# The 31-tap convolution of the forget-gate mixer: two of four channel tiles as blocked matmuls from shifted copies

## The reference, cut to what matters

```python
def conformer_conv(p_d, dw_w, dw_b, cn_g, cn_b):
    h = p_d[..., :D_D] * jax.nn.sigmoid(p_d[..., D_D:])
    h = causal_dwconv(h, dw_w) + dw_b
    h = layer_norm(h, cn_g, cn_b)
    return jax.nn.silu(h)

def odd_mixer(x, w_in, forget_b, dw_w, dw_b, cn_g, cn_b, w_out):
    p = x @ w_in
    ...
    log_f = jax.nn.log_sigmoid((p[..., 3 * D_C:3 * D_C + H_C] + forget_b).astype(jnp.float32))
    y_c = forgetting_attention(q, k, v, log_f).reshape(bsz, s, D_C)
    y_d = conformer_conv(p[..., 3 * D_C + H_C:], dw_w, dw_b, cn_g, cn_b)
    return jnp.concatenate([y_c, y_d], axis=-1) @ w_out
```

## Time and profile before

| | us |
|---|---|
| Median of 3 runs (2263.66 to 2265.57) | 2264.3 |
| The profiled execution | 2262.41 |
| Its span, first to last instruction | 2260.6 |
| TensorE busy | 2217.2 |
| VectorE busy | 1095.9 |
| ScalarE busy | 780.9 |
| GpSimd busy | 1002.0 |

### The profile page before, as it was taken

One profiled execution on the slowest core, in us unless ns is written; L12 is line 12 of the kernel. 1 busy time (PEld: TensorE's weight loads), 2 busy tenths in 40 slices (PEclk: granted clock), 3 DMA queues, 4 the chain that ended last, 5 costly groups with the idle time before them and its releaser, 6 DMA issues.

```text
span 2260.6 us, 25021 instructions
## 1 busy us (share of the span) xinstructions
PE 2217.2 (98%) x10111; PEld 1787.7 (79%) x10111; DVE 1095.9 (48%) x1693; ACT 780.9 (35%) x1033; POOL 1002.0 (44%) x318
## 2 busy tenths in 40 slices
PE   8999999999999999999999999999999999999998
PEld 6667888888777778888878888888878667888887
DVE  7535034455467451444557321444569725035455
ACT  2453223332344332333322232333336573223331
POOL 3223445554332343554545644536533334444553
PEclk9999999999999999999999999999999999999999
DMA  4122333232212222333333332333313113234332
GB/s 176 57 94 93 131 112 116 108 140 103 93 60 91 75 103 84 130 131 118 116 112 106 113 112 92 120 124 130 131 50 117 66 57 122 105 114 145 105 116 78
DMA packets 36994, 239.91 MB, mean 106 GB/s; under 512 B 4104, under 2 KB 5256, under 8 KB 10384
## 3 DMA queue, kind: packets, MB, share of 16 engines
q1 hardware_dynamic: 35712, 236.20, 29.1%
q10 hardware_dynamic: 1168, 2.11, 0.3%
HBM read 236.18 MB, written 2.11 MB: 105 GB/s over the span
## 4 chain that ended last, share of the span: by engine, by line
PE 85%; DVE 11%; ACT 2%; issue 1%; POOL 1%; DMA 0%; DVEq 0%; SPq 0%; ACTq 0%
PE bank L1147 17%; PE bank L1149 16%; PE bank L1148 16%; PE bank L1447 4%; PE bank L1448 4%; PE bank L1446 4%; PE bank L1197 3%; PE bank L1199 3%; PE bank L1198 3%; DVE bank L2353 3%; PE bank L1342 2%; PE bank L1337 2%; PE bank L1338 2%; DVE X L1950 1%; PE bank L1659 1%
## 5 line engine op out<-in xcount | busy, mean ns | idle before, releaser
L974 POOL TENSOR_TENSOR wlo<-raw,whi 128x2048 fp32r<-128x2048 f32 (+4 forms) x152 | 713.7, 4698 | 578.9 <-ACT whi L573 569.0
L1147 PE MATMUL bank<-XH,whi 128*128 128x512 f32 x1720 | 678.1, 394 | 6.6 <-POOL wlo L1042 6.1
L1149 PE MATMUL bank<-XH,wlo 128*128 128x512 f32 x1720 | 670.8, 390 | 0.0
L1148 PE MATMUL bank<-XL,whi 128*128 128x512 f32 x1720 | 670.3, 390 | 0.0
L1147 PEld LDWEIGHTS bank<-XH,whi 128*128 128x128 f32 x1720 | 323.4, 188 | 87.3 <-issue 15.0
L573 ACT CAST whi<-raw 128x2048 fp32r<-128x2048 f32 (+4 forms) x152 | 289.0, 1903 | 297.7 <-PE bank L1147 162.2
L1149 PEld LDWEIGHTS bank<-XH,wlo 128*128 128x128 f32 x1720 | 323.3, 188 | 67.9
L1148 PEld LDWEIGHTS bank<-XL,whi 128*128 128x128 f32 x1720 | 323.6, 188 | 64.9
L1011 POOL TENSOR_TENSOR AL<-AS,AH 128x1024 fp32r<-128x1024 f32 x40 | 123.6, 3090 | 345.0 <-ACT AH L622 345.0
L2035 DVE TENSOR_TENSOR HF<-sil,bank 128x512 f32<-128x512 f32 x56 | 38.5, 688 | 457.8 <-PE bank L1149 457.8
L1446 PE MATMUL bank<-whi,AH 128*128 128x512 f32 x448 | 174.3, 389 | 0.0
(11 more groups left out here) (298 smaller groups left out, 2952.6 us busy)
## 6 DMA issues: line engine op xcount, KB each, us to landing
raw<-w_ffn_gu SPq DMA_DIRECT2D x88, 1024.0 KB, 4.9
raw<-w_ffn_st SPq DMA_DIRECT2D x56, 1024.0 KB, 4.9
GB<-gb SPq DMA_DIRECT2D x8, 1024.0 KB, 6.9
raw<-w_ffn_dn SPq DMA_DIRECT2D x8, 1024.0 KB, 5.0
raw<-w_diff_in SPq DMA_DIRECT2D x6, 1280.0 KB, 5.6
raw<-w_ev_in SPq DMA_DIRECT2D x6, 1024.0 KB, 5.0
raw<-w_od_in SPq DMA_DIRECT2D x4, 1536.0 KB, 6.4
raw<-w_mla_pair SPq DMA_DIRECT2D x4, 1088.0 KB, 5.6
```

The lines of the kernel that those rows point to most:

```text
L974: pool.tensor_tensor(wlo[:, off:off + size], raw[:, off:off + size], whi[:, off:off + size].bitcast(F32), ALU.subtract).then_inc(lo_ready, 1)
L1147: release(pe.matmul(out, whi[:, off:off + P], xh, start=start, stop=False))
L1148: pe.matmul(out, whi[:, off:off + P], xl, start=False, stop=False)
L1149: return pe.matmul(out, wlo[:, off:off + P], xh, start=False, stop=stop)
```

## The change

Tiles 0 and 1 now both go to TensorE, in another form, and tiles 2 and 3 stay with VectorE (62 taps in place of 93). For each of the two tiles ScalarE issues 16 DMAs (`spread_taps`) that copy `fz` into `ZS`: partition group j of 32 gets the channels of group g shifted by j tokens, for every g. GpSimd makes the weights (`tap_weights`): 32 blocks of 128 x 32, each four small diagonals one above the other, for four taps of 32 channels. TensorE then does 8 blocks of four plain f32 matmuls (`conv_blocks`), one for each group of 32 output partitions, each contracting four taps at once. The 32nd tap is zero. The diagonals, their ring, and the high and low parts of z and of the weights go.

The order changes with it. TensorE: GLU unit, tile 0, GLU unit, tile 1, three-tile unit. ScalarE: both copies of z with their 16 issues each ahead of the cast of the second GLU unit, the cast of the three-tile unit ahead of the gate rows. GpSimd: the weights behind the first and the second GLU unit, the three-tile unit ahead of `diagonal_biases(0)`. VectorE: no taps before glu(2), then 22, glu(3), 9, and 5, 6 and 6 ahead of the three copies; 14 are left for the slots. The LayerNorm's steps all stand one slot earlier (rows in 4 to 6, the scaling at the end of slot 7, columns in 8 and 9, Silu in 10). Constants and parameters gain the columns that `tap_weights` reads.

```diff
-GLU_BANKS = ((0, 1), (0, 1), (2, 0), (1, 2))
+GLU_BANKS = ((0, 1), (0, 1), (0, 1), (2, 3))
-DIAGONALS = 4
+BLOCKED = 2
+TAP_BLOCKS = 8
+SPAN = 4 * (TAP_BLOCKS - 1) + S
...
+        TD = [sb(f"TD{i}", [P, 32, 32], F32, idle) for i in range(BLOCKED)]
+        stack = cons[:, CCOL["stack"]:CCOL["stack"] + 32]
+        ZS = [sb(f"ZS{i}", [P, 4, SPAN], F32, idle) for i in range(BLOCKED)]
-        dg = [sb(f"dg{i}", [P, 2 * P], F32R, ph) for i in range(DIAGONALS)]
...
@@ ScalarE
-            def diagonals(ks):
-                for k in ks:
-                    if k >= DIAGONALS:
-                        act.wait_ge(dg_used, k - DIAGONALS + 1)
-                    d = dg[k % DIAGONALS]
-                    act.activation(d[:, 0:P], ident, ACT.Copy, scale=cwH[:, k:k + 1].bitcast(F32))
-                    act.activation(d[:, P:2 * P], ident, ACT.Copy, scale=cwL[:, k:k + 1]).then_inc(dg_ready, 1)
+            def spread_taps(i):
+                act.wait_ge(z_kept, i + 1)
+                for j in range(4):
+                    for g in range(4):
+                        act.dma_start(ZS[i][32 * j:32 * j + 32, g, :], fz[i][32 * g:32 * g + 32, j:j + SPAN]).then_inc(zs_in[i], 16)
...
-            act.wait_ge(gz_done, 1)
-            act.copy(fz[1][:, PADC:], bank[5][:]).then_inc(z_kept, 1)
-            act.wait_ge(gz_done, 2)
-            act.copy(fzH[:, PADC:], bank[6][:]).then_inc(z_high, 1)
-            act.wait_ge(cw_lo, 1)
-            diagonals(range(0, 20))
+            act.wait_ge(z_padded, 1)
+            for e, b in ((0, 6), (1, 5)):
+                act.wait_ge(gz_done, e + 1)
+                act.copy(fz[e][:, PADC:PADC + S], bank[b][:]).then_inc(z_kept, 1)
+                spread_taps(e)
             split_w()
...
             sigmoid(2)
-            diagonals(range(20, 24))
+            keep_conv(0, blocks_done, 1)
+            split_w()
             act.wait_ge(cum_ready, 1)
             act.dma_start(gate_rows, cum[:]).then_inc(rows_out, 16)
-            diagonals(range(24, TAPS))
             act.wait_ge(rows_out, 16)
             gate_biases(0)
-            keep_conv(1, conv_done, 1)
-            keep_conv(0, dg_used, TAPS)
-            split_w()
             sigmoid(3)
             split_w()
-            keep_conv(2, conv_done, 2)
+            keep_conv(1, blocks_done, 2)
+            keep_conv(2, conv_done, 1)
...
@@ GpSimd
-            split_w(4)
+            def tap_weights(i):
+                pool.tensor_tensor(TD[i][:], stack.unsqueeze(1).to_broadcast([P, 32, 32]),
+                                   pcol_block("taps", i).unsqueeze(2).to_broadcast([P, 32, 32]), ALU.mult).then_inc(td_ready, 1)
+            split_w(3)
+            tap_weights(0)
+            split_w()
+            tap_weights(1)
+            split_w()
...
             diagonal_biases(0)
-            split_w(2)
+            split_w()
             diagonal_biases(1)
...
@@ TensorE
-            def conv_taps(ks):
-                for k in ks:
-                    pe.wait_ge(dg_ready, k + 1)
-                    d, z = dg[k % DIAGONALS], slice(k, k + S)
-                    pe.matmul(bank[7][:], d[:, 0:P], fzH[:, z], start=k == 0, stop=False)
-                    pe.matmul(bank[7][:], d[:, 0:P], fzL[:, z], start=False, stop=False)
-                    pe.matmul(bank[7][:], d[:, P:2 * P], fzH[:, z], start=False, stop=k == TAPS - 1).then_inc(dg_used, 1)
+            def conv_blocks(i):
+                b = CONV_BANK[i]
+                pe.wait_ge(td_ready, i + 1)
+                pe.wait_ge(zs_in[i], 256)
+                claim(b)
+                for k in range(TAP_BLOCKS):
+                    for g in range(4):
+                        ins = pe.matmul(bank[b][32 * g:32 * g + 32, :], TD[i][:, 4 * k + g, :], ZS[i][:, g, 4 * k:4 * k + S],
+                                        start=k == 0, stop=k == TAP_BLOCKS - 1)
+                ins.then_inc(blocks_done, 1)
...
-                for e, b in ((1, 5), (0, 6)):
+                for e, b in ((0, 6), (1, 5)):
...
             tile_end(ins, 2)
-            pe.wait_ge(z_low, 1)
-            claim(7)
-            conv_taps(range(0, 16))
             unit_into(GLU_BANKS[2])
-            conv_taps(range(16, TAPS))
-            freed[3], freed[4], freed[5], freed[7] = ((conv_kept, n) for n in (4, 1, 3, 2))
+            conv_blocks(0)
             unit_into(GLU_BANKS[3])
+            conv_blocks(1)
+            freed[7], freed[4], freed[5], freed[3] = ((conv_kept, n + 1) for n in range(4))
             unit_into((0, 6, 7))
...
-                if s in (6, 7):
-                    rows_of((1, 3)[s - 6])
-                if s in (9, 10):
-                    cols_of((0, 2)[s - 9])
+                if s in (5, 6):
+                    rows_of((1, 3)[s - 5])
+                if s in (8, 9):
+                    cols_of((0, 2)[s - 8])
...
@@ VectorE
-            taps_left = [(i, k) for i in range(1, 4) for k in range(TAPS)]
+            taps_left = [(i, k) for i in range(BLOCKED, 4) for k in range(TAPS)]
...
-            dve.wait_ge(z_high, 1)
-            dve.tensor_tensor(fzL[:, PADC:], bank[6][:], fzH[:, PADC:].bitcast(F32), ALU.subtract).then_inc(z_low, 1)
-            dve.wait_ge(z_kept, 1)
-            taps(3)
             take(lambda: dve.tensor_scalar(lfz[:], bank[2][0:8, :], parm[0:8, PCOL["f_b"]:PCOL["f_b"] + 1], None, ALU.add))
             link(dve.memset(lf0[:], 0.0))
-            taps(21)
...
-            taps(TAPS - 24)
             glu(2)
-            taps(TAPS)
+            taps(22)
             glu(3)
+            taps(TAPS - 22)
...
             for t in range(3):
-                taps((0, 2, 5)[t])
+                taps((5, 6, 6)[t])
                 copy_tile((fVT, fQ[0], fK[0])[t][:], (0, 6, 7)[t])
...
@@ host
+    dw = np.concatenate([f(inp["od_dw_w_2"]).reshape(TAPS, D // 2), np.zeros((4 * TAP_BLOCKS - TAPS, D // 2), np.float32)])
+    blocked = [dw[:, i * P:(i + 1) * P].reshape(TAP_BLOCKS, 4, 4, 32).transpose(1, 3, 0, 2).reshape(P, 32) for i in range(BLOCKED)]
+    con[:, CCOL["stack"]:CCOL["stack"] + 32] = p % 32 == np.arange(32)[None, :]
```

More of the change, by code:

```diff
@@ L59 @@
 PADC, PADW = TAPS - 1, 16
-PADDING = (56, 136)
+PADDING = (56, 104)
 PCOL, _n = {}, 0
 for _name, _w in (("g_c", 5), ("g_sub", 1), ("conv_w", 12), ("pool_s", 4),
-                  ("dw_w", 4 * TAPS), ("dw_b", 4), ("cn_g", 4), ("cn_b", 4), ("lam", 4), ("f_b", 1)):
+                  ("dw_w", (4 - BLOCKED) * TAPS), ("dw_b", 4), ("cn_g", 4), ("cn_b", 4), ("lam", 4), ("f_b", 1), ("taps", 32 * BLOCKED)):
     PCOL[_name] = _n
@@ L69 @@
 CCOL, _n = {}, 0
-for _name, _w in (("ident", P), ("dist", S), ("causal", P), ("invcnt", 64), ("slopes", 8)):
+for _name, _w in (("ident", P), ("dist", S), ("causal", P), ("invcnt", 64), ("slopes", 8), ("stack", 32)):
     CCOL[_name] = _n
@@ L271, in build @@
         idle = ExitStack()
+        TD = [sb(f"TD{i}", [P, 32, 32], F32, idle) for i in range(BLOCKED)]
+        idle.close()
+        idle = ExitStack()
         mPT1 = sb("mPT1", [P, NB, S], F32, idle)
@@ L396, in build @@
         fVT = sb("fVT", [P, S], F32, ph)
-        idle = ExitStack()
-        fB1 = [sb(f"fB1{m}", [P, S], F32, idle) for m in range(2)]
-        idle.close()
-        dg = [sb(f"dg{i}", [P, 2 * P], F32R, ph) for i in range(DIAGONALS)]
+        fB1 = [sb(f"fB1{m}", [P, S], F32, ph) for m in range(2)]
         idle = ExitStack()
@@ L404, in build @@
         cum = sb("cum", [8, S], F32, ph)
[L405 to L412, removed]
+        fz = [sb(f"fz{i}", [P, PADC + S + 2], F32, ph) for i in range(4)]
+        fYL = sb("fYL", [P, 2, S], F32R, ph)
         partmax = sb("partmax", [P, 4], F32, ph)
@@ L479, in build @@
         z_kept = sem("z_kept")
[L480 to L485, removed]
+        zs_in = [sem(f"zs_in{i}") for i in range(BLOCKED)]
+        z_padded = sem("z_padded")
+        td_ready = sem("td_ready")
+        blocks_done = sem("blocks_done")
         conv_done = sem("conv_done")
@@ L838, in sigmoid @@
                 tiles.add(2)
-            act.copy(cwH[:], parm[:, PCOL["dw_w"]:PCOL["dw_w"] + 4 * TAPS:4]).then_inc(cw_hi, 1)
             split_w()
@@ L927, in _ @@
                     odd_high(p - 1)
-                if s in (6, 7):
-                    keep_rows((1, 3)[s - 6])
-                if s in (9, 10):
-                    keep_cols((0, 2)[s - 9])
+                if s in (5, 6):
+                    keep_rows((1, 3)[s - 5])
+                if s in (8, 9):
+                    keep_cols((0, 2)[s - 8])
                 for m in range(2) if s else ():
                     keep_p(fPT[m], 6 + m, (s - 1) % 4)
-                if s == 5:
-                    keep_conv(3, conv_done, 3)
-                if s in (5, 6):
-                    keep_rows((0, 2)[s - 5])
-                if s == 8:
+                if s == 4:
+                    keep_conv(3, conv_done, 2)
+                if s in (4, 5):
+                    keep_rows((0, 2)[s - 4])
+                if s == 7:
                     act.wait_ge(cn_ready, 1)
```

(16 more changed lines are left out.)

32 lines of the change are left out of this document (16 added, 16 removed).

## The result

The kernel after takes 2277.59 us (median of 4 runs, 2277.20 to 2278.37) against 2264.94 for the kernel before: a ratio of 1.0058 (1.0046 to 1.0070), slower by 12.7 us. The forecast was 2264.1 with a range to 2271, so it was wrong by 13.5 us and outside its range. The profiled execution took 2277.68 us with a span of 2275.9, 15.3 us longer than the span of before.

The account below looks back on a forecast made before the run. It took VectorE's taps up to the fK copy, nearly level with TensorE's path, to bound slot 0. Terms +2.1 + 1.65 - 2.2 + 1.3 - 3.1 = -0.2 us against the 2264.3 median gave 2264.1 us, range 2257 to 2271.

Parts of the forecast that it names:

- ScalarE's queue: Before the second GLU weights' cast: 32 issues at 0.47 us replace the diagonals; cast starts at 1705.5, 0.7 us later.
- signs of being wrong: Cast before 1701 or after 1710, a tile's matmuls over 15 us, or attention starting over 4 us from 1756.7.
- rival 2: ScalarE's queue: issues hold it longer, 0.68 us each, fK 6.7 us later, 2270.8 us in all; chance 0.14.
- Rival 1: ScalarE's queue: issues cheaper than 0.47 us; at 0.33 us, 2259.6 us in all; chance 0.27.
- VectorE's part decides: Before slot 0: no taps until glu(2), then 48; fK at 1756.6, slot 0 starts 2.1 us later.
- The clock term: TensorE at slot 0: lower clock after about 10 us idle costs +1.65 us; bounds nothing to twice that.
- After slot 0: Attention slots: slot 4's three waits vanish, -2.2; slot 8 late, +1.3; slots 12 and 13 together, -3.1 us.
- the -3.1 at slots 12 and 13: Silu group a slot earlier: slot 13's 2.41 us wait and 1.65 us low clock go, slot 12 waits 1.0.
- The sum of -0.2: Whole kernel: +2.1 + 1.65 - 2.2 + 1.3 - 3.1 = -0.2 us against the median of 2264.3.
- the blocks run four side by side: TensorE's convolution: four 32-column groups overlap, so a tile costs 6.9 us and TensorE gains 7.7 us.
- two levelled paths at slot 0: Slot 0: TensorE and VectorE nearly level; a shorter TensorE path is worth nothing unless VectorE's taps end sooner.
- Rival 3: Column groups not four at a time: in pairs +2 us, one by one 2293 us; chance 0.09 together with late copies.

Follow-up runs that it names:

- e7_probe: Kernel before with 48 DMAs added at the end of ScalarE's list, eight of each of six kinds; its total time means nothing, only the trace was wanted.
- e1_sp: Kernel after with all 32 copies issued by SyncE instead of ScalarE: 2257.48 us against 2264.01 before, ratio 0.9970.
- e2_half: Kernel after with half of the issues (8 of 16 per tile) on SyncE and half on ScalarE: 2266.77 us, ratio 1.0014.
- e3_taps: Kernel after with GpSimd's second tap_weights moved ahead of the second GLU unit's wlo: 2275.63 us, ratio 1.0048.
- e6_best: Kernel after with SyncE's issues, both tap_weights ahead of the second GLU unit's wlo, LayerNorm steps in their slots of before: 2253.51 us, ratio 0.9955.
- e4_fill: Kernel after with 80 transposes of a constant added on TensorE behind the three-tile unit, before slot 0: 2273.10 us, ratio 1.0044.
- e8_serial: e1_sp with the loops of conv_blocks exchanged, so each column group's eight matmuls run in a row: 2287.12 us, ratio 1.0101.
- e10_one: Kernel after with only tile 0 by blocks, 16 issues by SyncE, tiles 1 to 3 on VectorE, LayerNorm's slots of before: 2266.53 us, ratio 1.0013.

## Why the prediction was wrong

**The step that failed is "ScalarE's queue".** It took 0.47 us per issue from a series of loads out of DRAM; these 32 copy out of SBUF and took 0.64 us a step, 0.68 on average, so the cast of the second GLU weights came 7.0 us later than forecast (1714.04, less the 1.6 us by which this profile ran late, against 1705.5). Two of the prediction's own signs of being wrong came with it: the cast after 1710, and the attention 11.1 us from 1756.7. The mechanism was there: rival 2 named it, at 0.68 us, and gave 2270.8 for it. It got 0.14, because I reasoned that a quarter of the bytes should cost less. e7_probe shows that bytes and partitions hardly enter. e1_sp and e2_half show that each issue on ScalarE moves slot 0. The Trainium skill, "DMA: Bandwidth & Descriptors", section "Issuing engines are not separate DMA queues", calls the time to initiate a DMA usually small beside the transfer; here 0.64 us stands against 2.1 us to landing in the middle of the 32 and 7.4 at most, and the 22 us that they hold the queue are longer than any of the transfers. Rival 1, which that sentence favoured, fell.

**"VectorE's part decides" was right, and its sum 2.8 us short.** The 48 taps took the forecast 0.79 us each and fK decided slot 0. What was missing is that lfu and lfc took 1.62 and 2.29 us instead of 0.42 and 0.68. I costed `tap_weights` at nothing because GpSimd was idle, and didn't ask whom a working GpSimd holds. Nor did I ask it of the wlo, which before was over (1711.42) when lfu had barely begun. e3_taps shows it for lfc directly, and lfu ends 0.28 us behind the wlo in after, e1_sp, e3_taps and e6_best, whether it takes 1.62, 1.73 or 2.79 us. In the forecast itself the end of the scan, 1715.1, was right by luck: it left out that the cast would be 0.7 us later, and took VectorE's delay there as 0.58 us, where lfu had begun 1.4 us behind the end of ScalarE's lfe. The Trainium skill has the rule, "SBUF — State Buffer", section "SBUF: two separate sides": VectorE and GpSimd share a port pair, and whichever starts first keeps it for the whole instruction, if VectorE's has two SBUF inputs or runs in a two-port mode. The trace agrees for lfc, which reads two tiles in SBUF, and for the taps, whose second input is in PSUM: 27 of the 60 ran beside a GpSimd instruction, and none took over 0.76 us. Which mode lfu ran in no trace says.

**The clock term** was 1.65 us and came to 2.3 (e4_fill), inside its bounds. The row it was read from followed an idle time of 2.4 us; behind 10.5 us the clock is still at its lower level from 1768 to 1773 us (granted 0.53). A second such stretch behind the 7.2 us wait made the second GLU unit 13.1 us long (1720.56 to 1733.69) instead of 10.9; that cost nothing, since VectorE decided.

**After slot 0** the forecast was -4.0 us beside slot 0's low clock; the trace has 107.69 - 2.3 - 105.67 = -0.3. Up to slot 8 it was near: -1.9 for -2.2 (50.1 us in e4_fill, 52.0 before). But of slot 4's three waits only 0.99 and 0.45 went. V's transposes still wait 0.67 us there, and a wait of 0.38 us in slot 6 that I hadn't counted went instead. From slot 8 on it was -1.8 and came to +1.6 (55.28 against 53.71): slot 8's wait was 1.5 for 1.3, and the -3.1 at slots 12 and 13 is the other step that failed. Two things were wrong in it. The two table loads moved from one place where TensorE waits for them to another: I followed them to the copies of P and not to the exponentials, the reciprocal and the fK copy behind it. And the low clock didn't go with the wait of slot 13: it now stands in slot 12, granted 0.50 from 1853 to 1856 us.

The sum of -0.2 is put right by +9.6 on the way to slot 0 (11.7 where +2.1 was forecast; the issues' 7.0 and VectorE's 2.8 by the rows), +0.6 for the clock, +3.7 for the slots and +1.6 ahead of the region: 15.3 us, the difference of the two spans.

**Right:** the blocks run four side by side, 6.9 us a tile (the 2.2 us over 1280 columns give 0.88 and not 0.86 for 512, but 0.86 is what e8_serial shows); two levelled paths at slot 0, so that a shorter TensorE path is worth nothing alone (e10_one).

**Right by luck:** the idle time before slot 0, 10.3 us forecast and 10.5 found. Both paths came over 9 us late, TensorE's by its 7.2 us wait and the low clock behind it, VectorE's by the issues and GpSimd, and the difference stayed. The copies were in time, but by a hair: the last of tile 0 landed at 1705.98, 4.2 us after its issue, and TensorE took it up at 1706.26, where the forecast had 3.6 us to spare.

Rival 3 fell, with e8_serial as its counter-proof: with the groups one after another a tile does cost more than 15 us, and slot 0 is late.

## What to carry to other kernels

Count every DMA issue as an instruction of the engine that issues it, at the price of a row with the same source, and let a queue issue whose next duty is far off: in this kernel the same 32 transfers cost 20 us more on ScalarE than on SyncE. When work is moved to an idle engine, ask which neighbour its instructions hold, and take a term as gained only after following the delayed instruction to the last one behind it.

## What the runs showed that was not expected

- The issue of a transfer out of SBUF takes ScalarE's queue 0.64 to 0.66 us, whatever its size from 32 x 512 bytes to 128 x 2160; out of DRAM it takes 0.47 to 0.48, tried with rows of 2160 bytes on 32 and 128 partitions (e7_probe). SyncE takes 0.63 for SBUF (e1_sp).
- With groups one after another a tile took 22.5 us and not four times the 6.9 of the interleaved order (e8_serial).
- The profiles differ ahead of the edited region by up to 3.5 us (first column of the table), through short stretches at the lower clock (1.2 GHz) that some executions have and others don't. The same stretch in the profiles of after and before:

```profile
66.50:69.00 2.50, 2.50 (x11) 2.31 (x12) 1.79 (x7) 0.88 (x4) 0.00 (x0) 0.50 0.00 0
```

```profile
66.50:69.00 2.50, 2.50 (x13) 2.04 (x13) 1.75 (x4) 1.02 (x4) 0.00 (x0) 1.00 0.00 0
```

In both TensorE had been busy for 4.36 of the 6 us from 60 to 66 us, at the upper level. What sets it off stays open. It moves this kernel by some 1.5 us a time, so differences of 2 us between medians were read from the stretches and not from the totals.
